# Handing out the matrix products around a blocked triangular inverse: one big product in single tiles between the halves of each level

## What is computed

```python
# delta net, per head, direction and chunk of 64 rows
a = jnp.where(strict, jnp.einsum('bhnld,bhnsd->bhnls', kb, k) * lmask, 0.0)
t = lax.linalg.triangular_solve(a + eye, ..., lower=True, unit_diagonal=True)
u = t @ (v * beta);  wk = t @ (kb * exp(gc))
# then a recurrence over 4 chunks, in both directions
v_new = u_c - w_c @ state
state = state * exp(gl_c) + ks_c.T @ v_new
# neighbourhood ("window") attention, 6 heads: softmax(q k^T + bias) v
# mLSTM ("memory" in the kernel's names), 4 heads: running maxima, states, gathered outputs
# cross-attention: kk, vv = split(rmsnorm(mem) @ w_kv)
```

## Time and profile before

| what | value |
|---|---|
| median of 3 runs | 1039.89 us (1039.2 to 1042.53) |
| the profiled execution's own time | 1040.62 us |
| its span, first to last instruction | 1038.9 us |
| mean granted TensorE clock | 0.990 |
| PE busy | 1018.3 us (98%) |
| DVE busy | 747.8 us (72%) |
| ACT busy | 571.2 us (55%) |

### The profile page before, as it was taken

The page is one execution under the profiler, slowest core; times in us unless marked ns, Lnnn a source line. Parts: engine busy times, 40 slices in busy tenths (PEclk is TensorE's granted clock), DMA queues, the critical chain, the costliest instruction groups (busy, mean ns, idle before and its releaser), DMA issues.

```text
span 1038.9 us, 21750 instructions
## 1 busy us (share of the span) xinstructions
PE 1018.3 (98%) x9147; PEld 936.6 (90%) x9147; DVE 747.8 (72%) x1188; ACT 571.2 (55%) x841; POOL 73.2 (7%) x177
## 2 busy tenths in 40 slices
PE   9999999999999999999999999889999999999997
PEld 8878999999977999999998899779899899998885
DVE  5879677788877966788899868846778466555445
ACT  5775575444666658544468565125345456575333
POOL 8700000000000000011140000000000000000000
PEclk9999999999999999999999999989999999999999
DMA  9656554455664545448787350001355355555552
GB/s 319 185 180 178 150 158 131 144 181 174 189 183 134 148 139 161 123 150 244 161 203 206 109 167 24 24 23 51 116 174 178 129 155 182 177 183 186 193 189 81
DMA packets 73553, 160.57 MB, mean 155 GB/s; under 512 B 6917, under 2 KB 16320, under 8 KB 73456
## 3 DMA queue, kind: packets, MB, share of 16 engines
q1 hardware_dynamic: 70304, 150.59, 46.9%
q0 software_dynamic: 2832, 8.06, 3.9%
q10 hardware_dynamic: 320, 0.53, 0.1%
HBM read 158.11 MB, written 1.05 MB: 153 GB/s over the span
## 4 chain that ended last, share of the span: by engine, by line
PE 92%; DVE 4%; ACT 2%; issue 1%; ACTq 0%; POOL 0%; DVEq 0%; POOLq 0%
PE psum L470 25%; PE psum L472 24%; PE psum L471 24%; PE psum L883 2%; PE psum L1035 2%; PE psum L872 1%; PE psum L724 1%; PE psum L702 1%; DVE ring_lo L1389 1%; DVE arena L1575 1%; PE psum L1309 1%; PE psum L716 1%; PE psum L1326 1%; PE psum L706 1%; PE psum L758 1%
## 5 line engine op out<-in xcount | busy, mean ns | idle before, releaser
L1389 DVE TENSOR_TENSOR ring_lo<-ring,ring_hi 128x1024 fp32r<-128x1024 f32 (+4 forms) x291 | 342.7, 1195 | 172.2 <-ACT ring_hi L2447 170.5
L2447 ACT ACTIVATE ring_hi<-ring 128x1024 fp32r<-128x1024 f32 (+4 forms) x291 | 297.8, 1034 | 265.9 <-PE psum L472 246.7
L470 PE MATMUL psum<-hT,ring_hi 128*128 128x256 f32 x904 | 258.1, 285 | 0.1
L472 PE MATMUL psum<-hT,ring_lo 128*128 128x256 f32 x904 | 255.3, 282 | 0.0
L471 PE MATMUL psum<-hT,ring_hi 128*128 128x256 f32 x904 | 254.9, 282 | 0.0
L470 PEld LDWEIGHTS psum<-hT,ring_hi 128*128 128x128 f32 x904 | 172.0, 190 | 2.6 <-issue 2.0
L472 PEld LDWEIGHTS psum<-hT,ring_lo 128*128 128x128 f32 x904 | 172.1, 190 | 0.0
L471 PEld LDWEIGHTS psum<-hT,ring_hi 128*128 128x128 f32 x904 | 172.0, 190 | 0.0
L470 PE MATMUL psum<-ring_hi,hT 128*128 128x512 f32 (+4 forms) x416 | 156.6, 376 | 1.2 <-DVE ring_lo L1389 0.6
L472 PE MATMUL psum<-ring_hi,hT 128*128 128x512 f32 (+4 forms) x416 | 152.5, 367 | 0.0
L471 PE MATMUL psum<-ring_lo,hT 128*128 128x512 f32 (+4 forms) x416 | 152.2, 366 | 0.0
(11 more groups left out here) (461 smaller groups left out, 1361.6 us busy)
## 6 DMA issues: line engine op xcount, KB each, us to landing
ring<-in_w_in SPq DMA_DIRECT2D x104, 512.0 KB, 3.6
ring<-in_w_ff SPq DMA_DIRECT2D x64, 512.0 KB, 3.5
ring<-in_w_branch SPq DMA_DIRECT2D x24, 512.0 KB, 3.7
ring<-in_w_out SPq DMA_DIRECT2D x24, 512.0 KB, 3.4
ring<-in_w_in SPq DMA_DIRECT2D x24, 384.0 KB, 3.2
ring<-in_w_xkv SPq DMA_DIRECT2D x16, 512.0 KB, 3.7
ring<-in_w_in SPq DMA_DIRECT2D x8, 528.0 KB, 4.0
ring<-in_w_xq SPq DMA_DIRECT2D x8, 512.0 KB, 3.7
```

Of the source, the lines that this page charges most:

```text
L470: mm(b, lhs[0], rhs[0], start=start, stop=False, **how)
L472: return mm(b, lhs[1], rhs[0], start=False, stop=stop, **how)
L1389: V.tensor_tensor(chunk_view(ring_lo, RAW, c), chunk_view(ring, RAW, c), plain(chunk_view(ring_hi, RING_HI, c)), ALU.subtract).then_inc(ev ...
L2447: AC(chunk_view(ring_hi, RING_HI, c), chunk_view(ring, RAW, c), ACT.Copy).then_inc(ev("whi_ready"), 1)
```

## The change

The last column slot and the keys of xk 0 and xk 1 are handed out in smaller pieces, in other places, and the small stages around them change their order on all three engines:

- cols_steps can stop after each half of a chunk, T_steps after each tile, and T_steps asks before each chunk only for that chunk's slice of memT.
- p2 slot 5 keeps its last chunk back: its first half is issued after inv0 and ao (which move in front of it with mlrow, mlT and memT 0, 1), its second half between the halves of level 1.
- The sixteen tiles of xk 0 are issued as 1 (between the halves of level 2), 2, 1 (level 3), 2 after memory_scores, 1 (level 4), 1 after memory_states and the window heads, 1 (level 5), 2, 4 after the window scores(0), and the last one behind state_write(0). Those of xk 1 as 4, 2, 2, 4, 4 in the recurrence.
- window_heads moves from before level 2 to behind level 4, window_scores(0) from behind level 4 to the end of the inverse, window_scores(1), the napT transposes and the napv products into the recurrence; no chunk of xv 0 is left in the recurrence, all four follow oi and oa.
- DVE and ACT follow in their programs: among others lo_until(43) stays before window_maxima(0) and new_values(0), the second scaled_keys moves between the two mlstm_gathered, window_maxima(1) and mlstm_out move behind new_state(0), and ACT's memory_k(0) moves behind hi_until(44), memory_k(1) behind hi_until(48).

No instruction of the computation is added or removed. The core of the diff:

```diff
-            def cols_steps(tag, lhs, parts=1, first=False):
+            def cols_steps(tag, lhs, parts=1, first=False, by_row=False):
...
+                        if by_row and t < T - 1:
+                            yield c
...
-            def T_steps(tag, rhs, tiles=4):
+            def T_steps(tag, rhs, tiles=4, by_tile=False, ready=None):
                 names = [(*tag, g) for g in range((tiles + 1) // 2)]
                 banks = hold(names)
                 for c in range(CHUNKS):
+                    if ready:
+                        ready(c)
...
+                        if by_tile and f < tiles - 1:
+                            yield c
...
-            p2(5, {0: key_products(1), 1: query_products})
-
-            turn[0] += 6
-            memory_rows()
-            p2_copied(1, 2)
-            for t in range(T):
-                turns(("mlT", t), [proj2[:, t, C_MLQ + k * P:C_MLQ + (k + 1) * P] for k in range(4)])
-
...
+                if between:
+                    between()
...
+            def inverse_begun():
+
+                turn[0] += 6
+                memory_rows()
+                p2_copied(1, 2)
+                for t in range(T):
+                    turns(("mlT", t), [proj2[:, t, C_MLQ + k * P:C_MLQ + (k + 1) * P] for k in range(4)])
+                memory_turns(0, 1)
+                pe.wait_ge(ev("inv0_ready"), 1)
...
+            last_columns = cols_steps(("p2", 5), hT, by_row=True)
+            for stage in (None, key_products(1), None, query_products, None, inverse_begun):
+                next(last_columns)
+                if stage:
+                    stage()
+            next(last_columns)
+
...
+            def tiles(steps, n):
+                for _ in range(n):
+                    next(steps)
+
+            keys = T_steps(("xk", 0), hT, by_tile=True, ready=lambda c: copied(pe, ("memT", c)))
+            inverse_level(1, lambda: next(last_columns))
             memory_turns(2, 3)
             memory_maxima()
+
+            def first_tile():
+                turn[0] += 4
+                tiles(keys, 1)
+                turn[0] += 2
+
+            inverse_level(2, first_tile)
+            tiles(keys, 2)
+            inverse_level(3, lambda: tiles(keys, 1))
+            memory_scores()
+            tiles(keys, 2)
+            inverse_level(4, lambda: tiles(keys, 1))
+            memory_states()
             window_heads()
-            copied(pe, *[("memT", g) for g in range(4)])
-            keys = T_steps(("xk", 0), hT)
-            next(keys)
-            inverse_level(2)
-            next(keys)
-            inverse_level(3)
-            memory_scores()
-            memory_states()
-            inverse_level(4)
-            copied(pe, *[("naT", t, q) for t in range(T) for q in range(2)])
-            window_scores(0)
-            next(keys)
+            tiles(keys, 1)
+            inverse_level(5, lambda: tiles(keys, 1))
             memory_products(0)
+            tiles(keys, 2)
             memory_products(1)
-            inverse_level(5)
-            window_scores(1)
-            run(keys)
-            held.update(where[("xk", 0, g)][0] for g in range(2))
             delta_decays()
             delta_factors(0)
             delta_factors(1)
-            let_go([("xk", 0, g) for g in range(2)])
-
-            window_turns(0)
-            window_turns(1)
-            for t in range(T):
-                copied(pe, *[("napT", t, q) for q in range(3)])
+            copied(pe, *[("naT", t, q) for t in range(T) for q in range(2)])
+            window_scores(0)
+            tiles(keys, 4)
+            copied(pe, *[(n, t, d) for n in ("gu2", "gw") for t in range(T) for d in range(2)])
+
+            def window_values(t):
+
+                copied(pe, *[("napT", t_, q) for t_ in range(T) for q in range(3)])
...
-            keys, values = T_steps(("xk", 1), hT), cols_steps(("xv", 0), hT)
+            more_keys, values = T_steps(("xk", 1), hT, by_tile=True), cols_steps(("xv", 0), hT)
             state_write(0, 0)
             state_write(0, 1)
-            next(keys)
+            run(keys)
+            window_scores(1)
+            tiles(more_keys, 4)
+            window_turns(0)
             state_read(1, 0)
             state_read(1, 1)
-            next(keys)
+            tiles(more_keys, 2)
+            window_turns(1)
             state_write(1, 0)
             state_write(1, 1)
-            next(keys)
+            tiles(more_keys, 2)
             state_read(2, 0)
             state_read(2, 1)
-            next(keys)
+            window_values(0)
             state_write(2, 0)
             state_write(2, 1)
+            window_values(1)
+            state_read(3, 0)
+            state_read(3, 1)
+            tiles(more_keys, 4)
             copied(pe, ("napv", 0), ("napv", 1))
             mixed_turns("na", 0, 3)
-            next(values)
-            state_read(3, 0)
-            state_read(3, 1)
+            run(more_keys)
             pe.wait_ge(ev("mlstm_mixed"), 1)
             mixed_turns("ml", 3, 5)
-            next(values)
...
-            lo_until(40)
+            lo_until(39)
             memory_low(0)
             memory_low(1)
             running_maxima()
+            window_mask(0)
             inverse_level(1, 0)
             inverse_level(1, 1)
             memory_low(2)
             memory_low(3)
             mlstm_decays()
+            lo_until(40)
             copied(dve, *[("p2", i, t, 0) for i in (1, 2) for t in range(T)])
             mlstm_values()
-            dve.wait_ge(ev("zt_ready"), 1)
-            vf(V.scalar_tensor_tensor(out=z2, in0=zt, scalar=1.0, in1=z2, op0=ALU.add, op1=ALU.mult), "dve")
-            window_mask(0)
-            window_mask(1)
-            lo_until(41)
             inverse_level(2, 0)
             inverse_level(2, 1)
             mlstm_keys()
-            scaled_keys(0)
-            lo_until(42)
             inverse_level(3, 0)
             inverse_level(3, 1)
             mlstm_scores()
-            mlstm_states()
+            lo_until(41)
             inverse_level(4, 0)
             inverse_level(4, 1)
-            scaled_keys(1)
-            window_maxima(0)
-            lo_until(43)
-            mlstm_gathered(0)
-            mlstm_gathered(1)
+            dve.wait_ge(ev("zt_ready"), 1)
+            vf(V.scalar_tensor_tensor(out=z2, in0=zt, scalar=1.0, in1=z2, op0=ALU.add, op1=ALU.mult), "dve")
+            mlstm_states()
+            copied(dve, *[("naT", t, q) for t in range(T) for q in range(2)])
+            scaled_keys(0)
+            lo_until(42)
             inverse_level(5, 0)
             inverse_level(5, 1)
-            window_maxima(1)
-            mlstm_out()
-            dve.wait_ge(ev("w_ready"), 1)
-            vf(V.tensor_tensor(z2, z2, bc(gd_w, 1, T), ALU.mult))
-
+            mlstm_gathered(0)
+            scaled_keys(1)
+            mlstm_gathered(1)
+            window_mask(1)
+            lo_until(43)
+            window_maxima(0)
             copied(dve, *[(n, t, d) for n in ("gu2", "gw") for t in range(T) for d in range(2)], "gdec2")
             vf(V.memset(gd_st[:, 0, :, :, :], 0.0))
             new_values(0, 0)
@@ -2267,28 +2288,30 @@
             lo_until(44)
             new_state(0, 0)
             new_state(0, 1)
-            window_out()
+            window_maxima(1)
+            mlstm_out()
             new_values(1, 0)
             new_values(1, 1)
+            lo_until(45)
             new_state(1, 0)
-            lo_until(45)
             new_state(1, 1)
-            lo_until(46)
+            dve.wait_ge(ev("w_ready"), 1)
+            vf(V.tensor_tensor(z2, z2, bc(gd_w, 1, T), ALU.mult))
             new_values(2, 0)
             new_values(2, 1)
+            lo_until(46)
             new_state(2, 0)
-            lo_until(47)
             new_state(2, 1)
-            lo_until(48)
-            low_mixed("na", 0, 3)
+            window_out()
             new_values(3, 0)
             new_values(3, 1)
-            lo_until(49)
+            lo_until(47)
+            low_mixed("na", 0, 3)
+            lo_until(48)
             low_mixed("ml", 3, 5)
             delta_out(0)
+            delta_out(1)
             lo_until(50)
-            delta_out(1)
-            lo_until(51)
             head_norm(gd_o, GNH, 640, z2, "mixed_ready")
             lo_until(55)
...
-            p2(5)
-            hi_until(40)
             copy_out("mlrow", ml_row[0:MLH, :, :, :].rearrange("p q d n -> p (q d n)"), 1024, rows_=MLH, banks=2)
             turned_memory_heads(0)
             turned_memory_heads(1)
@@ -2839,12 +2860,11 @@
             moved_factors(1)
             inverse_level(1, 0)
             inverse_level(1, 1)
+            p2(5)
+            hi_until(40)
             memory_high(2)
             memory_high(3)
             copy_out("mlcol", ml_col[:, :, :, :].rearrange("p q t n -> p (q t n)"), 48)
-            turned_window_heads(0)
-            turned_window_heads(1)
-            hi_until(41)
```

(29 more changed lines are left out.)

40 lines of the change are left out of this document (18 added, 22 removed).

## The result

The changed kernel took 1052.74 us (median), the kernel before in the same rounds 1041.15 us; the ratio of the runs is 1.0106 [1.0092, 1.0120], 11 us. Measured again later, the two gave 1.0118 [1.0084, 1.0151]. One of the changed kernel's six executions took 2117.73 us, for a reason that I don't know; the ratio compares fast executions only and leaves it out (the median of the other five is 1052.71). The forecast was 1046.4 with a range of 1038 to 1052, so the measured time lies 0.7 us above the range: the sign and the places of the waits were right, and the loss of 11.6 us was 1.8 times the forecast's 6.5.

What follows compares the result with a forecast made beforehand. PE was taken as the bound, a matmul in flight for 98% of the span. Idle 15.3 - 11.0, switches 1.4, fetching 1.5, clock 0 gave +7.2, taken as +6.5 on 1040.62; median 0.7 lower: 1046.4 us, range 1038 to 1052.

Steps and rivals of the forecast that it cites:

- 4, state_write(0): PE waits at state_write(0) for new_values(0), queued on DVE behind chunk 42's low part and window_maxima(0): 3.1 us.
- 5, window_scores(1): PE waits at window_scores(1) for an xk 0 bank that memory_k(0) empties behind chunk 43's high part: 2.5 us.
- 6, napT and state_read: Third napT bank, emptied by new_values(1, 0) behind window_maxima(1) and mlstm_out; partly at state_read(1, 1): 3.3 us in all.
- 7, "oi": First "oi" waits for the banks of xk 1, as memory_k(1) is queued behind hi_until(48): 1.8 us.
- I take 2 us off (bounds 0 and 5): PE's own delays before a wait shorten it: 2 us off the waits' 17.3, leaving 15.3 us of idle time.
- Clock: "no difference": Lost clock from 620 to 755 us: bounds 0 to 10 us, taken as 6.8 as before, so 0 added.
- Switches: PE has 21 pieces of chunk products instead of 14, at 0.2 us each: 1.4 us (bounds 0.7 and 2.1).
- Fetching: PE's gaps without a semaphore: none to 3.8 us, taken as 1.5 with tiles inside the levels.
- I take +6.5: Whole time: the terms' sum gave +7.2 us, the schedule laid end to end +6; +6.5 was taken.
- no change: Rival: new waits are there, but fetching gaps and lost clock go altogether: -1.1 us, 1038.8 us; chance 0.14.
- faster: Rival: clock stays at 2.4 GHz through the inverse, no fetch is seen, new waits under about 11 us: 1033.2 us; chance 0.10.
- much slower: Rival: nothing absorbed, fetching stays, one more half-clock stretch of 7 us: +14.9 us, 1054.8 us; chance 0.08.

Runs made afterwards that it cites:

- e1: Changed kernel with chunk 42's low part on DVE behind window_maxima(0) and new_values(0), its high part on ACT behind window_exp(0): 1048.28 us, ratio 1.0075.
- e4: Changed kernel, PE's program the same, with lo_until(43), its high part and mlstm_out moved, memory_k(0), memory_k(1) before their high parts: 1042.15 us, ratio 1.0003.
- e8: Changed kernel's inverse with the old recurrence; both window_scores, napT and napv between them: 1043.18 us, ratio 1.0022.
- e6: e4 with memory_low(0), (1) and the z2 product earlier on DVE, four tiles before window_scores(1), two behind it: 1042.89 us, ratio 1.0015.
- e9: e8 with both window_scores and the last keys in front of delta_decays and delta_factors: 1040.75 us, ratio 1.0014.
- e11: e10 with two key tiles between the window scores, three behind them, and window_maxima(1) in front of low part 42: 1041.70 us, ratio 1.0008.
- e5: Kernel before with 64 extra four-column matmuls and 64 weight loads at the program's start: 1052.31 us, one run.
- e10: e9 with memory_low(0), (1) in front of DVE's low part 38 and the z2 product in front of level 3: 1042.96 us, ratio 1.0026.

## Why the prediction missed its range, and what in it held

The mechanism held: the loss is bank and data waits behind the in-order queues of DVE and ACT. The size did not: 1052.74 us lies above the range that ended at 1052. Each wait, as forecast and as measured in the changed kernel's first profile:

| step | forecast us | measured us |
|---|---|---|
| 1, bank of "ao" | 1.8 | 1.1 |
| 2, window heads | 1.9 | 1.1 |
| 3, delta_decays | 1.7 | 1.2 + 0.3 |
| 4, state_write(0) | 3.1 | 3.4 |
| 5, window_scores(1) | 2.5 | 2.4 |
| 6, napT and state_read | 3.3 | 2.4 + 0.9 + 0.4 |
| 7, "oi" | 1.8 | 1.8 |
| small ones | 1.2 | 2.4 |
| sum | 17.3 | 17.4 |

- *What the change takes away* was right: the semaphore waits and fetching gaps of before are not in the new list, but for short ones that I counted anew.
- *Waits* were right in place; 3 to 7 came within 0.4 us of their size, 1 and 2 at some 60% of it. e1 to e4 show the cause for 4, 5, the 2.4 us of 6, and 7 (1.8 us, and 0.9 at the same place in e4). **A step that failed is "I take 2 us off (bounds 0 and 5)".** The semaphore waits came to 17.2 us on the mean of three profiles, not 15.3. I had measured each wait from PE's own last instruction in front of it, so that earlier delays of PE were in it already; taking them off again counted them twice. That is my reading of how I had worked; no run isolates it. And that the plain sum of 17.3 met the measured one so well is in part luck: the seven named waits were 1.1 us shorter than forecast and the small ones 1.2 us longer. Miss: 1.9 us.
- *Clock: "no difference"* was mis-sized by as much, and is the other step that failed. The clock lost was 6.7, 10.4 and 8.0 us against 6.5 and 6.3 before, on the mean 2.0 more. The bounds (0 to 10 us) held it, the value did not: I had named the new half clock behind waits 4 to 6 as the upper bound and then taken "what was" for the value, with no reason for the new one to stay away or the old one in the inverse to go. The old one went in the first execution only, and some 10 us of a new one stood behind waits 4 and 5 in all three.
- *Switches* were right as far as this can be read: busy time rose by 3.4 us on the mean (141.8 to 145.1), less 2.0 of clock leaves 1.4 us for 1.4 forecast; e4 has 1.7.
- *Fetching* was right on the mean, but by luck: 1.6 us for 1.5, against 4.5 before, with single profiles at 2.6, 1.0 and 1.3. I forecast the smaller gaps for the tiles inside the levels, and that cause was not shown: the gap differs from 0 to 2.3 us at the same instruction, and e8, e6 and e9, which all have tiles inside, had 0.1, 3.6 and 4.8 us in all.
- *"I take +6.5"* instead of the sum's 7.2 cost another 0.7, with no row behind it.

Together: 6.5 + 1.9 + 2.0 + 0.7 = 11.1 us, where the stretch grew by 11.0 on the mean of the profiles (163.95 less 152.99) and the medians by 11.6. A last 1.3 us of the time itself is no step of the forecast: the kernel before measured 1041.15 us here, and I had started from 1039.89. By that alone 1052.74 is above 1052 and not below it, so the miss of the range is a narrow one, while that of the size (11.6 for 6.5) is not. One sign that I had named as proof against me, a clock of 1.00 from 637 to 700 us, was there in the first profile though the rest held, and not in the second. It was a bad sign: it belongs to the execution. The other held: the four gaps at 4 to 7 were 10.0 us together, and 6 was the bar.

The rivals: "no change" and "faster" fell with the waits; "much slower" (1054.8) was near in time, and right in that nothing is absorbed, but wrong on fetching. Of the Trainium skill's Perfetto Trace Analysis (Optimization Strategy) the first half was seen in part: with interleaving the inverse's part was shorter by 3.3 to 4.8 us, and the waits behind it, with the clock lost after them, took that back more than threefold. The other half, that repeated bubbles can mean too few buffers, fits less: the waits were mostly for banks, but each came once, and e4 was rid of 6.5 us of them with the same eight banks. Not settled is whether some order keeps the gain, and whether the tiles are what brought it. Twelve orders were tried; the best (e4, e9, e11) cannot be told from the kernel before, and none is faster.

## What to carry to other kernels

When a product is cut into tiles and laid between other stages, walk the in-order queues of the *other* engines: the first instruction there that needs the product's later tiles holds everything behind it, and a few lines moved on DVE and ACT were worth 10.6 us here. If the forecast walks PE's queue wait by wait from PE's own last instruction, add the waits up and take nothing off without a row for it; here the plain sum was 17.3 us and 17.2 were measured, though its terms missed in both directions. When one wait is taken away, look for the next for the same engine before counting a gain, and repeat a profile before reading anything from a fetching gap or the place of a half-clock stretch.

## What the hardware showed that I had not expected

- PE ran dry at fixed counts of its records, every 256, in stretches of dense 64x64 products, for 0.2 to 2.3 us, at other edges not at all. The Trainium skill (Runtime: NRT & Kernel Launch, Instruction fetch mechanics) has blocks of 256 instructions, which agrees; it has the refill mostly hidden, and here it cost 0 to 3.7 us in this stretch.
- 64 matmuls of only four columns, each with its 128x128 float32 weight load, ran 10.94 us, 171 ns each, with the granted clock at 0.50 from 10 us on although PE was never idle. In e5:

```profile
5.97 10.94 PE L652 MATMUL psum<-ones 128*128 128x4 f32 x64
```

```profile
10.00:20.00 10.00, 10.00 (x48) 9.94 (x48) 0.94 (x3) 1.73 (x5) 8.69 (x25) 0.50 0.99 333
```

- The same kernel lost 6.7 to 10.4 us of clock in different executions, and outside the stretch the span's remainder moved from 883.9 to 888.8 us between profiles (e5 left out) in which PE's work there is the same; this is why kernels whose semaphore waits differ by 3 us (e8 with 13.0, e10 with 9.7) are not told apart by their times.
